# Order of products, copies, loads and waits around the first gather of a pool-mixer and PEER kernel

## What is computed

```python
# first block: pool mixer, then layer norm
h = x @ w_in ; u, z = split(h)                       # w_in 1024 x 4096
m = einsum(window_means(u) - u, w_grp) * scale
x = layer_norm(ALPHA * x + (m * silu(z)) @ w_out)
# second block
h = modulate(rmsnorm(x, norm1_g), sh1, sc1)
gate_b, gate_c, xa, xr, gr = split(h @ w_in2)
y = concat(head_rmsnorm(y_a), head_rmsnorm(y_b)) @ w_out2
x = x + g1 * y
h = modulate(rmsnorm(x, norm2_g), sh2, sc2)
# PEER, per token: 8 heads, 16 experts each
q = h @ w_q ; sc = einsum(q, sub_keys)               # two halves, 128 keys each
top 16 of each half, top 16 of the 256 sums -> idx, g = softmax(best)
act = gelu(expert_u[idx] . h)
x = x + g2 * sum((g * act) * expert_v[idx])
return rmsnorm(x, final_g)
```

## Time and profile before

| what | us |
|---|---|
| median of 3 runs (1789.92 to 1790.77) | 1790.66 |
| the profiled execution | 1784.64 |
| its span, first to last instruction | 1782.8 |
| PE busy | 1574.0 (88%) |
| DVE busy | 1382.0 (78%) |
| POOL busy | 822.7 (46%) |
| ACT busy | 705.3 (40%) |
| gathers: 512, POOL busy with them | 799.5 |

### The profile page before, as it was taken

How to read it: one execution, slowest core, us unless ns; L and a number is a source line. 1 busy time by engine, 2 the same in 40 slices (tenths; PEclk the granted TensorE clock), 3 DMA queues, 4 the chain that set the end, 5 groups by cost and what they waited for, 6 DMA issues and landing times.

```text
span 1782.8 us, 20466 instructions
## 1 busy us (share of the span) xinstructions
PE 1574.0 (88%) x4830; PEld 818.4 (46%) x4830; DVE 1382.0 (78%) x3013; ACT 705.3 (40%) x2000; POOL 822.7 (46%) x554
## 2 busy tenths in 40 slices
PE   9999999999999888888888888888888888888887
PEld 7888878777544433333333333333333333333332
DVE  5788977677688887778777777887777788777777
ACT  6222423546143443333433343343333334333333
POOL 2000000000144446665566767556766656576763
PEclk9999999999999999999999999999999999999999
DMA  6565572331499999999999999999999999999996
GB/s 245 193 229 175 198 275 80 134 132 60 160 380 421 421 421 421 421 420 413 422 422 421 422 422 422 421 422 423 422 422 421 422 422 422 422 423 422 422 422 289
DMA packets 92995, 620.72 MB, mean 348 GB/s; under 512 B 11392, under 2 KB 11408, under 8 KB 23568
## 3 DMA queue, kind: packets, MB, share of 16 engines
q0 software_dynamic: 77936, 566.81, 77.1%
q1 hardware_dynamic: 14864, 53.00, 8.2%
q10 hardware_dynamic: 144, 0.26, 0.0%
HBM read 617.94 MB, written 2.10 MB: 348 GB/s over the span
## 4 chain that ended last, share of the span: by engine, by line
PE 35%; DMA 30%; POOL 12%; issue 9%; DVE 8%; DVEq 3%; ACT 3%; POOLq 0%; ACTq 0%; SPq 0%
DMA arena<-in_experts,idx 28%; POOL arena L451 12%; PE ps L703 9%; PE ps L462 7%; PE ps L463 7%; PE ps L464 7%; DVE arena L1556 4%; PE ps L639 2%; PE ps L605 2%; DMA arena<-in_w_in 1%; DVEq L1374 1%; ACT arena L966 1%; ACT stats L964 1%; PE ps L572 0%; ACT lnw L962 0%
## 5 line engine op out<-in xcount | busy, mean ns | idle before, releaser
L703 PE MATMUL ps<-arena 128*128 128x512 f32 x2048 | 998.4, 616 | 195.5 <-ACT arena L966 185.8
L451 POOL DMA_INDIRECT arena<-in_experts,idx x512 | 799.5, 1561 | 637.2 <-issue 371.8
L703 PEld LDWEIGHTS ps<-arena 128*128 128x128 f32 x2048 | 356.0, 191 | 789.3 <-ACT arena L966 518.1
L1556 DVE CUSTOM_DVE_ANT_0 arena<-arena,ada 128x1024 f32<-128x1024 f32 x448 | 548.7, 1225 | 178.7 <-DMA arena<-in_experts,idx 173.2
L962 ACT ACTIVATE lnw<-lnw 128x1 f32<-128x1 f32 x512 | 103.7, 203 | 696.5 <-DVE lnw L1556 695.9
L966 ACT ACTIVATE arena<-ident,stats 128x128 f32<-128x128 f32 x512 | 205.5, 401 | 36.6 <-issue 0.7
L964 ACT ACTIVATE stats<-lnw 128x1 f32<-128x1 f32 x512 | 150.8, 295 | 35.8 <-issue 0.7
L414 POOL DMA_DIRECT2D arena<-in_w_ada x24 | 12.7, 530 | 221.2 <-DVE ada L1089 216.5
L1556 DVE CUSTOM_DVE_ANT_0 arena<-arena 128x1024 f32<-128x1024 f32 x64 | 78.0, 1219 | 12.8 <-DMA arena<-in_experts,idx 12.4
L1089 DVE SCALAR_TENSOR_TENSOR ada<-arena,cact,ada 128x512 f32<-128x512 f32 x96 | 72.2, 752 | 17.4 <-DMA arena<-in_w_ada 9.7
L462 PE MATMUL ps<-xT_hl,w_hl 128*128 128x512 f32 x192 | 75.4, 393 | 1.9 <-DVE xT_hl L1055 1.2
(11 more groups left out here) (273 smaller groups left out, 1734.9 us busy)
## 6 DMA issues: line engine op xcount, KB each, us to landing
arena<-in_w_ada POOLq DMA_DIRECT2D x24, 1024.0 KB, 5.7
arena<-in_w_in SPq DMA_DIRECT2D x43, 512.0 KB, 3.3
arena<-in_experts,idx POOLq DMA_INDIRECT x512, 14.7
arena<-in_w_out SPq DMA_DIRECT2D x14, 512.0 KB, 5.4
lnw<-in_w_in SPq DMA_DIRECT2D x8, 512.0 KB, 4.0
arena<-in_w_grp POOLq DMA_DIRECT2D x4, 1024.0 KB, 8.9
arena<-in_w_out SPq DMA_DIRECT2D x1, 4096.0 KB, 13.2
arena<-in_w_q SPq DMA_DIRECT2D x1, 4096.0 KB, 13.6
```

The lines of the kernel that those rows point to most:

```text
L451: nc.gpsimd.indirect_dma_start(slot(n), None, experts, bass.IndirectOffsetOnAxis(ap=idx[:, e, n:n + 1], axis=0)).then_inc(arr[n % RING], 16)
L703: last = mm(ps[half][:, :], lhsT=diag[:, n % RING, :], rhs=slot(n)[:, DM + half * T:DM + (half + 1) * T], start=(e == 0 and n == 0), stop= ...
L1556: nc.vector.tensor_tensor_reduce(out=urow, in0=urow, in1=rows, scale=1.0, scalar=0.0, op0=ALU.mult, op1=ALU.add, accum_out=dots[:, e, n:n ...
```

## The change

- SP: the load of xT pieces 4 and 5 no longer waits for piece 0; pieces 6 and 7 wait for piece 0 instead of piece 1; chunk 1 waits for piece 1.
- POOL: the wait for a free place stands ahead of the wait for the indices, not behind it.
- PE: the fifth product of tile 1 (half 0, n = 4) stands ahead of the transposes of h2. `query(1)` follows `score(0)` at once, and `score(1)` follows three products later. Ten products of tile 2 (before: three) and the sixteen of tile 3 stand in the expert loop, at every second slot from 8 to 38 and at each from 39 to 48.
- ACT: `copy_score(1)` stands ahead of the tanh and no longer waits for `idx_ready`; the copy of query 1 still precedes both. `late_rows` and `late_root` move. `ACT_SLOT` goes from 104 to 105.
- DVE: the fifteen entries of `late_h2` move to later slots. At the end the lower half is scaled by root and gain in one operation; its own product with the gain is gone.

```diff
-FIRST_LATER, LATE2 = 6, 3
+LATE2 = 10
+LATE_SLOTS = tuple(range(8, 40, 2)) + tuple(range(39, 49))
...
-DVE_SLOT, ACT_SLOT = 88, 104
+DVE_SLOT, ACT_SLOT = 88, 105
...
             sp.dma_start(raw_of(0)[:, T:], w_in[0, 0, :, T:]).then_inc(raw_arr[0], 16)
+            load_xT(4, 2)
             sp.wait_ge(xT_in[0], 16)
-            load_xT(4, 2)
+            load_xT(6, 2)
             sp.wait_ge(xT_in[1], 16)
-            load_xT(6, 2)
             load_chunk(1)
...
                     for n in range(TOPK):
+                        pool.wait_ge(slot_free, 2 * TOPK * i + TOPK * e + n + 1)
+                        pool.sem_inc(pool_go, 1)
                         if n % EIGHT == 0:
                             pool.wait_ge(idx_ready, 4 * i + 2 * e + n // EIGHT + 1)
                             pool.sem_inc(pool_go, 1)
-                        pool.wait_ge(slot_free, 2 * TOPK * i + TOPK * e + n + 1)
-                        pool.sem_inc(pool_go, 1)
...
             pe.wait_ge(gc_copied, NJ)
-            for n in range(4):
+            for n in range(5):
                 wout2_mm(1, 0, n)
...
             score(0)
-            for n in range(4, 6):
-                wout2_mm(1, 0, n)
+            query(1, ps[1][:, 0:P])
+            wout2_mm(1, 0, 5)
             pe.wait_ge(v_ready, NJ)
-            for n in range(6):
+            for n in range(2):
+                wout2_mm(1, 1, n)
+            pe.wait_ge(q_copied, 2)
+            pe.wait_ge(score_ready, 2)
+            score(1)
+            for n in range(2, 6):
                 wout2_mm(1, 1, n)
             pe.wait_ge(yT_ready, 2 * NJ + 2)
             for half in range(2):
                 for n in range(6, 8):
                     wout2_mm(1, half, n)
-            query(1, ps[1][:, 0:P])
-            pe.wait_ge(ya_ready, NJ)
-            wout2_mm(2, 0, 0)
-            pe.wait_ge(q_copied, 2)
-            pe.wait_ge(score_ready, 2)
-            score(1)
-            for n in range(1, 5):
-                wout2_mm(2, 0, n)
             pe.wait_ge(score_ready, 4)
             query(2, query_out(2))
-            for n in range(5, 7):
+            pe.wait_ge(ya_ready, NJ)
+            for n in range(2):
                 wout2_mm(2, 0, n)
             pe.wait_ge(q_copied, 3)
             score(2)
-            wout2_mm(2, 0, 7)
-            for n in range(KD - LATE2):
-                wout2_mm(2, 1, n)
+            for n in range(2, 2 * KD - LATE2):
+                wout2_mm(2, 0, n)
...
+            copy_score(1)
             act.wait_ge(best_ready, 1)
             nc.scalar.activation(best[:, :], best[:, :], ACT.Tanh, scale=0.5).then_inc(half_tanh, 1)
-            act.wait_ge(idx_ready, 2)
-            copy_score(1)
             copy_q(0, query_out(0), 3)
-            late_rows = {(0, 12): 1, (2, 2): 2, (3, 0): 3}
-            late_root = (3, 2)
+            late_rows = {(1, 0): 1, (2, 2): 2, (3, 8): 3}
+            late_root = (3, 9)
...
-            late_h2 = {(0, 1): (1, 0), (0, 3): (1, 1), (0, 8): (1, 2), (0, 13): (1, 3),
+            late_h2 = {(0, 9): (1, 0), (0, 11): (1, 1), (0, 13): (1, 2), (0, 15): (1, 3),
...
-            for half in range(2):
-                c = slice(half * T, (half + 1) * T)
-                dve.drain()
-                tt(lastb[:, c], outb[:, c], fing[:, c], ALU.mult).then_inc(last_scaled, 1)
+            dve.drain()
+            tt(lastb[:, T:], outb[:, T:], fing[:, T:], ALU.mult).then_inc(last_scaled, 1)
             dve.wait_ge(root_ready, 4 * NT)
             nc.vector.reciprocal(stats[:, 14:15], stats[:, 14:15]).then_inc(inv_ready, 1)
             dve.drain()
-            ts(lastb[:, 0:T], lastb[:, 0:T], stats[:, 14:15], None, ALU.mult).then_inc(low_half, 1)
+            stt(lastb[:, 0:T], outb[:, 0:T], stats[:, 14:15], fing[:, 0:T], ALU.mult, ALU.mult).then_inc(low_half, 1)
```

More of the change, by code:

```diff
@@ L1017, in _ @@
             root_of_halves()
-            act.wait_ge(last_scaled, 2)
+            act.wait_ge(last_scaled, 1)
             act.wait_ge(inv_ready, 1)
```

10 lines of the change are left out of this document (5 added, 5 removed), and 6 rows, old and new, of the table late_h2.

## The result

| | kernel before | kernel after |
|---|---|---|
| first set, median (lowest to highest) | 1789.92 (1788.44 to 1790.77), 5 runs | 1780.86 (1779.74 to 1781.89), 5 runs |
| profiled execution, its span | 1784.64, 1782.8 | 1780.86, 1779.0 |
| another chip, later, 28 and 7 runs | 1785.16 (1783.99 to 1786.52) | 1780.07 (1779.74 to 1781.41) |

The ratio of the later chip is 0.9973 (0.9962 to 0.9984): 5.1 us. The profiled execution was forecast at 1780.6 and took 1780.9. The error lies in the step from there to the median.

What follows compares the result with a forecast made beforehand. The expert gathers' DMA stream at 421 GB/s was taken as the bound. Hole -4.0, extra product +0.45, POOL -0.2, first loads 0 and tail -0.27 sum to -4.0 us: median 1790.66 becomes 1786.6, range 1785.2 to 1789.2.

Steps and rivals of the forecast that it cites:

- extra product ahead of the transposes: PE, tile 1's fifth product before the h2 transposes: delays everything after it by 0.45 us, at best 0.35.
- POOL's order: POOL, slot wait put ahead of the index wait: one instruction less before the first gather, -0.2 us (-0.3 to 0).
- hole: Gather stream behind the eighth gather, 502 to 516 us: the ninth waits for a slot; closing it gives -4.0 (-3.3 to -4.5).
- tail: Final scaling: one gain product less, ACT's half, said to store last, sooner by 0.27 us; range -0.27 to -0.05.
- sum of the ends: The terms' extremes added: -2.7 us at one end (with 0.53 for the extra product) and -5.1 at the other.
- First loads: Start, xT and chunk 1 loads issued 0.4 to 0.9 us sooner: taken as 0, gain at most 0.4, loss at most 0.1.
- Products behind the diagonals: Expert loop, 26 products in slots 8 to 48: lateness hidden by the ring, taken at 0; uncovered some 1 to 2 us.
- The clock (rival 2): PE waits at the diagonals, its clock falls to 0.50 and a hole opens: only -1.8 us, 1788.8; chance 0.07.
- thin queue: Gather stream: hole closes, but six slots run at 356 GB/s with few gathers in flight: -1.7 us, 1789.0; chance 0.14.
- earlier loads: Start: first loads do arrive sooner, 1 us at the front, hole worth 4.5: -5.5 us, 1785.1; chance 0.06.
- The step that failed: From profiled execution (1784.64, becoming 1780.6) to the runs' median: 1790.66, 6.0 higher, becomes 1786.6, with 1785.6 to 1788.0.

Runs made afterwards that it cites:

- after_25_ahead: Kernel after with 25 products again between score(0) and the first diagonal; queries, tanh and h2 tables as in after: 1785.62 us, ratio 0.9978.
- before_ten_behind: Kernel before with only the products moved behind the diagonals (ten of tile 2) and their tables; queries, tanh and copies stay: 1786.75 us, ratio 0.9988.
- before_new_front: Kernel before with only the first loads reordered as in the kernel after: 1788.11 us, ratio 0.9995.
- after_again: Kernel after, unchanged, on a chip where the kernel before took 1785.16: 1780.07 us, ratio 0.9973.
- before_again: Kernel before, unchanged, run and profiled again: 1788.5 us; its profiled execution took 1790.46.
- before_hold: Kernel before, but POOL starts its first gather only when ACT has copied query 1: 1789.38 us, ratio 1.0.
- before_act_busy3: Kernel before with seventeen unused copies on ACT between the copies of query 0 and query 1: 1788.42 us, ratio 0.9999.
- before_slot120: Kernel before with ACT's instructions moved by 16 places (ACT_SLOT 104 to 120): 1788.05 us, ratio 0.9996.
- after_old_front: Kernel after with the old order of the first loads alone put back: 1780.41 us, ratio 0.9954.
- set A: Runs on one chip sharing runs of the kernel before, which took 1789.39 us there; query copy late in 4 of 4 profiles.
- sets A, B and E: Runs on three chips with late query copies (4 of 4, 4 of 4, 1 of 2 profiles); kernel before took 1789.39, 1788.95 and 1788.60 us.
- sets C and D: Runs on two chips without late query copies (0 of 4 profiles each); kernel before took 1785.25 and 1785.16 us.
- core_only: Kernel after with the old first loads, POOL order, tail and ACT_SLOT 104: 1780.8 us, ratio 0.9956.
- before_four_first3: Kernel before, but POOL issues four gathers and holds the fifth until ACT has copied query 1: 1785.24 us, ratio 0.998.

## Why the prediction was right and wrong

Point by point, from the profiled executions (span 1782.8 and 1779.0):

| step | forecast | measured | from |
|---|---|---|---|
| start of the dense part up to the last products | 0 | +0.42 in this pair | 455.55 to 455.97 |
| extra product ahead of the transposes | +0.45 | +0.30 | 19.76 and 20.06 us to score(0) |
| POOL's order | -0.2 | -0.18 | score(0) to first gather, 5.66 and 5.48 |
| hole | -4.0 | -4.3 | first gather to last dot product, 1290.13 and 1285.83 |
| tail | -0.27 | -0.04 | last dot product to the end, 11.70 and 11.66 |
| sum | -4.0 | -3.8 | |

- **Hole.** Right in place and cause. It has two causes that must both go, as after_25_ahead and before_ten_behind show. Forecast: first dot product 494.3, ninth gather 499.3; measured 494.8 and 500.3, of which 0.54 is the later first gather. None of the stretches shown of after lies under 416 GB/s.
- **Extra product.** 0.30, just under its range of 0.35 to 0.53: the transposes start 0.35 later (16.31 instead of 15.96 us behind the first of the products), as the lower bound had it, and 0.05 of that come back on the way to score(0). (The 0.53 in the sum of the ends should have been 0.51, 0.86 - 0.35.)
- **First loads.** The +0.42 is no step of the change. At the same point six profiles with the new order stand at 455.00 to 456.36, fourteen with the old at 455.23 to 456.18. Forecast 0, confirmed by before_new_front.
- **POOL.** Right.
- **Tail.** The mechanism was right and its effect mis-sized. Before, 8.13 us lie between the last dot product (1771.10) and ACT's scaling at 1779.23; after, 7.84 (1767.34 to 1775.18): 0.29 sooner. But the DVE's half, in one operation of 0.75 us in place of 0.49, ends only 0.03 us sooner, and the profile's chain of after ends with it (L1603), where that of before ended with ACT's half (L1020). The prediction said that ACT's half stores last; the bound -0.05 was the better value.
- **Products behind the diagonals.** Right at 0: 421 GB/s in 530 to 1750, as in the earlier trace rows.
- **The clock (rival 2).** In after_again the PE waited 0.66 us at the first diagonal (forecast 0.7) and kept its full clock of 2.4 GHz (1.00). The clock fell to 0.50 behind waits of 2.37 us (before_again), 2.82 (before_ten_behind) and 1.98 (before_hold, 0.50 in 502 to 504 us), and not behind the 2.29 us of before_act_busy3 and the 2.21 of before_slot120: the length of that one wait doesn't tell whether it falls. Where it did fall it was with the old order of queries, where the prediction hadn't looked for it: between before_again and before_act_busy3 it makes 1.7 us at the first diagonal product. The rivals of a thin queue and of earlier loads are out as well.
- **The step that failed** is "the median of the runs shown, 1790.66, lies 6.0 higher and becomes 1786.6". It carried the distance over as if it were a constant of measurement. It was the hole itself. Per profile, 50 x (421.4 - g)/421.4, with g the GB/s in 484 to 534 us and 421.4 GB/s the rate of before in 530 to 1750 us (514.06 MB in 1220 us), gives the time lost there:

| profile | g | lost, us | span |
|---|---|---|---|
| first profile of before | 385 | 4.3 | 1782.8 |
| before_new_front | 373 | 5.7 | 1785.0 |
| before_slot120 | 361 | 7.2 | 1786.5 |
| before_again | 341 | 9.5 | 1788.7 |
| after_25_ahead | 378 | 5.1 | 1784.1 |
| after | 419 | 0.3 | 1779.0 |
| after_old_front | 420 | 0.2 | 1778.6 |

Span less loss is 1778.4 to 1779.3 in all seven, and 1777.7 to 1779.5 in all twenty profiles: the hole accounts for the whole difference between the kernels and between the executions of one. What makes it deeper on three chips is the late signal of set A, which the prediction had no row of. Closing it therefore gains what it costs in the typical execution of that chip, 9 us or 5, and the time after is 1780 to 1781 on all. The sign of the trouble stood in the rows: three runs of 1789.9 to 1790.8 beside a profile of 1784.6 are two behaviours, not an offset, and the change removed the stretch in which the difference could lie. After forecasting a hole closed, the prediction should have asked how long the hole is in the runs that it had no trace of. Whether the first profile came from a chip without late copies or from a rare execution on one with them isn't known for certain: of the 85 runs of this kernel in the first set and in sets A, B and E, none is under 1785.5. One thing speaks for such a chip: the list of semaphore updates has 13667 to 13687 entries in the eight profiles of sets C and D, 13672 in this one, and 13457 to 13552 in the other eleven.

## What to carry to other kernels

Where the profiled execution lies well off the median, find out which stall differs before carrying the distance through a change; if the change removes that stall, the absolute time after is what the trace predicts, and the gain is whatever the stall costs in typical runs. A stall that needs two late engines to go asks for an experiment with each alone, and chip differences ask for runs of the old kernel in every set. When an engine starts late, see first when the signal that it waits for was given: here that put the lateness with another engine than the one that stood idle, and fits that making ACT busy and moving its instructions changed nothing. In a dense start-up, put the small operations that the first consumers need (here the copy of a query and the tanh) ahead of the burst of gathers, and don't rely on them inside it.

## What the runs showed of the hardware

On three of five chips the PE's signal that a query is done came 1.3 to 3.4 us behind the end of its last record while the first eight gathers were in flight, and ACT's copy with it: in 9 of 10 profiles there, and in none of 8 on the two other chips. The wait ended 8.5 to 8.6 us after the first gather (before_new_front, before_ten_behind, before_hold), 9.9 to 10.0 (before_again, before_slot120, before_act_busy3) or 11.5 to 11.7 (core_only, after_old_front, after_25_ahead, and after, whose chip isn't known). The signal of the score behind a late query 1 is late too, by 0.6 to 2.0 us. In the same stretch the recorded signals of ACT and of the DVE stand right behind their instructions, so only the PE's are touched. Shown: it goes with the first gathers (before_hold), needs no idle ACT (before_act_busy3), doesn't depend on a shift of ACT's instructions (before_slot120), and all but goes when only four gathers are issued before the copy (before_four_first3, one chip, one profile and 8 runs, all under the unchanged kernel's; query 2's signal is 0.27 us late there).

Open: what in the gathers does it, whether the PE's work or only its signal is late, and why only some chips. The list of DMA packets in the trace has an 8 KB instruction packet 5.9 to 6.8 us after the first gather in every profile with eight gathers, on both kinds of chip, and 12.0 us after it in before_four_first3; so that run moved both the fifth gather and this packet, and does not tell their effects apart. The traces of the three chips, and of after, also lack over a hundred entries of semaphore updates that the others have (13457 to 13552 against 13667 to 13687), so it is open too whether the recording takes part. No experiment changed what the PE signals.
